# A fused conv and MLP layer on one core: T2 is put onto R21 by an adding transfer in the first two turns

## The reference, cut to what matters

```python
def short_conv_mixer(h, w_in, conv_w, w_out):
    b_gate, c_gate, v = jnp.split(h @ w_in, 3, axis=-1)
    u = c_gate * v
    y = lax.conv_general_dilated(u, conv_w[:, None, :], window_strides=(1,),
        padding=[(CONV_WIDTH - 1, 0)], dimension_numbers=('NWC', 'WIO', 'NWC'),
        feature_group_count=d)
    return (b_gate * y) @ w_out

def squared_relu_mlp(h, w1, w2):
    a = jax.nn.relu(h @ w1)
    return (a * a) @ w2

x = x + short_conv_mixer(rmsnorm(x, mix_norm), conv_w_in, conv_w, conv_w_out)
x = x + squared_relu_mlp(rmsnorm(x, mlp_norm), mlp_w1, mlp_w2)
```

## Time and profile before

| | us |
|---|---|
| median of 3 runs | 1921.16 |
| lowest, highest | 1919.78, 1921.49 |
| the profiled execution, its own time | 1920.67 |
| its span, first to last instruction | 1918.9 |
| PE busy | 1888.6 |
| DVE busy | 1713.0 |
| ACT busy | 1024.4 |
| POOL busy | 152.4 |

### The profile page before, as it was taken

One profiled execution on the slowest core, in us unless ns is written; L12 is line 12 of the kernel. 1 busy time (PEld: TensorE's weight loads), 2 busy tenths in 40 slices (PEclk: granted clock), 3 DMA queues, 4 the chain that ended last, 5 costly groups with the idle time before them and its releaser, 6 DMA issues.

```text
span 1918.9 us, 22282 instructions
## 1 busy us (share of the span) xinstructions
PE 1888.6 (98%) x8512; PEld 1562.5 (81%) x8512; DVE 1713.0 (89%) x1510; ACT 1024.4 (53%) x1102; POOL 152.4 (8%) x244
## 2 busy tenths in 40 slices
PE   6999999999999999999999999999999999999999
PEld 5778888888888888888888888888888888888887
DVE  7989899898999989989899898998998889888878
ACT  6753655536557486565665656655444333333332
POOL 1100001000011111111111111110000000000000
PEclk9999999999999999999999999999999999999999
DMA  9866659657776975967858678599988878877782
GB/s 361 307 208 171 224 173 376 214 158 263 243 198 245 376 221 182 335 243 238 318 185 331 247 235 322 183 397 400 362 311 348 351 284 310 349 317 277 296 329 116
DMA packets 120698, 527.90 MB, mean 275 GB/s; under 512 B 13072, under 2 KB 17168, under 8 KB 95504
## 3 DMA queue, kind: packets, MB, share of 16 engines
q1 hardware_dynamic: 86176, 401.64, 54.5%
q0 software_dynamic: 34272, 124.80, 21.4%
q10 hardware_dynamic: 144, 0.04, 0.0%
HBM read 433.10 MB, written 93.32 MB: 274 GB/s over the span
## 4 chain that ended last, share of the span: by engine, by line
PE 91%; DVE 4%; ACT 2%; issue 2%; DMA 1%; POOL 0%; ACTq 0%; DVEq 0%
PE pair L1014 89%; PE pair L1034 2%; DVE ring L787 1%; DVE raw L781 1%; DMA act_kept<-act 1%; ACT ring L545 1%; DVE act L744 1%; DVE sum_l_mix L818 0%; ACT quads L497 0%; DVE sum L816 0%; ACT act L530 0%; DVE sum_first_mix L827 0%; DMA quads<-in_xt 0%; ACT u_pad L608 0%; ACT sum L571 0%
## 5 line engine op out<-in xcount | busy, mean ns | idle before, releaser
L1014 PE MATMUL pair<-ring,act 128*128 128x512 f32 x8064 | 1851.8, 391 | 23.5 <-DVE ring L787 17.5
L1014 PEld LDWEIGHTS pair<-ring,act 128*128 128x128 f32 x8064 | 1512.5, 188 | 340.0 <-issue 21.6
L545 ACT ACTIVATE ring<-raw 128x1024 fp32r<-128x1024 f32 x672 | 710.8, 1060 | 833.0 <-PE pair L1014 563.1
L787 DVE TENSOR_TENSOR ring<-raw,ring 128x1024 fp32r<-128x1024 f32 x672 | 808.5, 1220 | 149.3 <-ACT ring L545 146.7
L781 DVE TENSOR_TENSOR raw<-raw 128x1024 f32<-128x1024 f32 x324 | 381.7, 1219 | 8.0
L432 POOL DMA_DIRECT2D spill<-stage x136 | 78.2, 609 | 474.9 <-ACT stage L649 371.6
L445 POOL DMA_DIRECT2D raw<-in_turns x60 | 53.5, 1045 | 780.5 <-DVE raw L781 780.5
L768 DVE TENSOR_TENSOR stage<-quads,stage 128x1024 fp32r<-128x1024 f32 x68 | 82.9, 1219 | 25.7 <-ACT stage L649 25.0
L818 DVE TENSOR_TENSOR sum<-pair,sum 128x1024 f32<-128x1024 f32 x64 | 77.9, 1217 | 0.0
L649 ACT ACTIVATE stage<-quads 128x1024 fp32r<-128x1024 f32 x68 | 71.4, 1051 | 11.8 <-DVE quads L716 10.1
L571 ACT ACTIVATE sum<-pair 128x1024 f32<-128x1024 f32 x64 | 64.7, 1011 | 0.0
(11 more groups left out here) (91 smaller groups left out, 438.3 us busy)
## 6 DMA issues: line engine op xcount, KB each, us to landing
raw<-in_turns SPq DMA_DIRECT2D x192, 1024.0 KB, 7.2
act<-spill SPq DMA_DIRECT2D x282, 512.0 KB, 6.7
spill<-stage POOLq DMA_DIRECT2D x136, 512.0 KB, 9.2
act<-act_kept SPq DMA_DIRECT2D x68, 512.0 KB, 7.1
raw<-in_turns POOLq DMA_DIRECT2D x60, 512.0 KB, 8.6
act_kept<-act POOLq DMA_DIRECT2D x26, 512.0 KB, 11.2
x_tok<-in_x SPq DMA_DIRECT2D x4, 1024.0 KB, 12.7
x<-mixed SPq DMA_DIRECT2D x8, 512.0 KB, 16.1
```

What stands on the lines that cost most here:

```text
L545: nc.scalar.activation(ring[g % RING][:, 0], raw[:, RAW_OF[j], 2 * (s % 2):2 * (s % 2) + 2, :], ACT.Copy).then_inc(hi_ready, 1)
L787: nc.vector.tensor_tensor(ring[g % RING][:, 1], raw[:, RAW_OF[s // 2], 2 * (s % 2):2 * (s % 2) + 2, :], ring[g % RING][:, 0].bitcast(F32), ...
L1014: mm = nc.tensor.matmul(bank, stationary, moving, start=(opens and k == 0 and n == 0), stop=(closes and k == NT - 1 and n == 2))
```

## The change

A fourth kind of transfer is added. In turns 0 and 1 (`t4_by_transfer`) POOL issues, behind the kept copies of the turn, two transfers of 512 KB that read T2 from R11 in `raw` and add it onto R21 in `raw`, so that both ends are on the chip. They wait for T2 and for lo of slot 7. Each half has a semaphore, `t4_in0` and `t4_in1`. DVE's two operations for T4 are left out in these turns. Hi of slots 12 and 13 waits for the half that it reads, and SP's load of the next turn's R11 waits for both halves. All other turns stay as they are, only the count of formed sums is adapted.

```diff
+def t4_by_transfer(v):
+
+    return v < 2
...
+        t4_in = [sem("t4_in0"), sem("t4_in1")]
...
-            before = sum(3 if t3_by_transfer(w) else 4 for w in range(v))
+            before = sum(4 - t3_by_transfer(w) - t4_by_transfer(w) for w in range(v))
...
                     if r == R11:
-                        sp.wait_ge(t_formed, formed(v, T4))
+                        if t4_by_transfer(v):
+                            for half in range(2):
+                                sp.wait_ge(t4_in[half], 16 * (v + 1))
+                        else:
+                            sp.wait_ge(t_formed, formed(v, T4))
                         load_raw(after, r)
...
+            def add_t4(v):
+
+                pool.wait_ge(t_formed, formed(v, T2))
+                pool.wait_ge(lo_ready, SLOTS * v + 8)
+                for half in range(2):
+                    k = slice(2 * half, 2 * half + 2)
+                    pool.dma_start(raw[:, R21, k], raw[:, R11, k], accum_op=ALU.add).then_inc(t4_in[half], 16)
...
                     keep_act(3, S2, S4, L22)
+                if t4_by_transfer(v):
+                    add_t4(v)
                 if v > 1:
                     put_spills(v)
...
+                elif j == L22 and t4_by_transfer(v):
+                    act.wait_ge(t4_in[s % 2], 16 * (v + 1))
                 elif j == S3 and t3_by_transfer(v):
...
-                    if s == 7:
+                    if s == 7 and not t4_by_transfer(v):
                         form_weights(v, T4)
```

## The result

The changed kernel took 1923.36 us (median of 20 runs, 1922.27 to 1926.28), the kernel before 1920.90 us in the same comparison (20 runs, 1919.48 to 1922.78). The ratio is 1.0013, 95% interval 1.0008 to 1.0019: 2.5 us slower, a difference that 20 runs show but that is under the 0.2% (3.8 us) named in the prediction. The profiled execution of the changed kernel took 1922.53 us, its span is 1920.8 us.

A forecast was written before the change was run, and what follows sets the result against it. PE, 98% busy, was taken as the bound, following DVE from turn 1 to the start of turn 2. Terms -1.8, +2.4 and +2.1 gave +2.7 us on 1920.67, so 1923.4, forecast as median 1923.9; range 1918.1 to 1929.2.

The forecast's parts named there:

- within 0.2%: Whole kernel: a time within 0.2% (3.8 us) of the kernel before, given a chance of 0.60.
- the three terms: Turns 0 to 2: -1.8 (kept copies), +2.4 (R12 behind tokens), +2.1 (R11 of turn 2), together +2.7 us.
- The second term: Turn 0 into turn 1: R12, behind 2 MB of tokens, lands at 65.7 and holds up T1; +2.4 us.
- the price of an addition: New transfers in turns 0 and 1: each adding transfer of 512 KB was taken to cost 2.9 us in the queue.
- The sign that would have refuted the prediction: PE's slot 4 of turn 2 starting before 119; it was forecast at 120.2, from 117.47.
- The step that the argument hung on: Turn 1 into 2: R11 of turn 2, issued at 96.4, lands at 101.2; DVE's list behind comes 2.7 us later.
- The first: Rival for turns 0 and 1: additions cost 1.25 us each like copies; -3.1 us, 1918.1 us; chance 0.08.
- The second: Rival for turns 0 and 1: SP waits for dearer additions; at 4.2 us each +7.9, 1929.1 us; chance 0.33.
- Its rate: Four additions ahead of the next R11: each 0.1 us more on an addition is 0.4 us on the kernel.
- The third: Rival in turn 2: PE's slot 4 may not be its only bound; sum near 0, 1921.2 us; chance 0.12.

The follow-up runs named there:

- e1: The changed kernel with T4 by transfer in turn 0 alone; 1922.67 us against 1921.49 for the kernel before, ratio 1.0005.
- e5: The changed kernel with four of turn 1's kept copies moved behind T3's transfers of turn 2; 1921.17 us against 1921.03 before, ratio 0.9999.
- e3: The changed kernel with turn 0's two token loads behind R21 instead of R11; 1923.85 us against 1921.49 before, ratio 1.0014.
- e4: The kernel before, with only SP's load of R11 of turn 2 held until lo of slot 12 of turn 1; 1923.26 us against 1921.49, ratio 1.0011.
- e10: The kernel before, with a semaphore for each operand's pair of kept copies of turn 0; 1919.52 us against 1921.00, ratio 0.9991.
- e8: The changed kernel with T4 by transfer in turn 1 alone and four kept copies moved to turn 2; 1919.98 us against 1921.03 before, ratio 0.9995.
- e9: The four new transfers copy T2 over R21 instead of adding it, leaving out the sum; 1919.27 us against 1921.03 for the kernel before, ratio 0.9988.
- e11: e8 plus a semaphore for each pair of kept copies of turn 0; 1918.96 us against 1921.00 for the kernel before, ratio 0.9990.

## Why the prediction was right, point by point

**The sum.** +2.7 us were forecast; the medians say +2.5, the profiled executions +1.9 (1922.53 to 1920.67). The median was forecast as 1923.9 and is 1923.4, inside the range and inside "within 0.2%". The path was as forecast, term by term, but that the number is so close is in part luck. Counted from lo of slot 4 of turn 0, the three terms were -1.68, +1.21 and +1.64 in the changed kernel's trace, for -1.8, +2.4 and +2.1. They give +1.17, and the other 0.56 us at slot 4 of turn 2 is the later start of slot 4 of turn 0 in this execution. The second term is not steady: in e1 and e5, whose turn 0 is the same, R12 landed 1.4 and 1.3 us later in the turn, and the term was +2.7 and +2.6.

**Turn 0.** The kept copies did speed up once SP held its loads back: the last landed at 48.1 (issued at 39.5, 8.6 us), 47.7 was forecast, 53.5 before. ACT's wait went from 3.37 to 1.66, and ended at 52.44, when `direct_s` was done (51.13 + 1.23 = 52.36; the row itself names only "issue"), as the prediction said. The additions landed at 50.6 and 53.05 (50.6 and 53.5), R12 at 65.3 (65.7), DVE stood 1.32 us for it, and T1 of turn 1 started at 65.28 (65.8; 65.19 before). PE's slot 12 was at 58.30, not 57.6; lo of slot 4 of turn 0 was already 0.56 later in this execution (31.76 to 31.20). e3 and e1 show both halves of the account: 1.2 us less without the tokens ahead of R12, and the gain gone with them.

**Turn 1.** The last kept copy, issued at 73.8, landed at 90.2 (90.5), the additions at 92.7 and 95.2 (93.4 and 96.3). The **cost that was mis-sized is the price of an addition**, 2.5 us and not 2.9: four of them make 1.6 us, but the first pair shows in T1 only in part. The 2.9 came from one pair of T3 in one execution; in e4 and e10, which leave that pair as it is in the kernel before, it was 2.5. R11 was issued at 95.25 and landed at 100.1 (96.4, 101.2), lo of slot 0 started at 101.25 (102.2), lo of slot 4 at 117.92 (118.9), PE's slot 4 at 119.20 (120.2). The sign that would have refuted the prediction, a start before 119, was close.

**The step that the argument hung on**, that the late load of R11 and not the waits on slots 12 and 13 sets the end of turn 1, is shown by e4: with the load alone 42.9 us, with the whole change 42.8, and the same 17.8 us from hi of slot 0 to lo of slot 4. That VectorE's saving is worth 1.3 us and no more if nothing is late is shown by e5, e8, e9 and e11: 41.2 became 39.9 each time.

**The rivals.** The first, additions as cheap as copies, was wrong about the additions; the sum given for it, -3.1 at the join, came near, as e9 showed by making them copies: 113.42 at slot 4 of turn 2, 2.8 us ahead of before; of this the median kept 1.8. The second, dearer additions, did not come: they were cheaper than in either row of T3, with SP's loads held back. Its rate, 0.4 us on the kernel for each 0.1 us, has only the two ends of e9 and the changed kernel behind it: 4.2 us (each against its own before) for 1.25 us less on each, so 0.34 for each 0.1. The third, a delay that doesn't reach the end, fell: ACT's wait before `sum_l_mix` stayed (0.63 for 0.67), and the 1.73 us at slot 4 of turn 2 became 1.86 at the end.

The Trainium skill's fit for a transfer ("DMA: Bandwidth & Descriptors", "Anatomy of one DMA — SWDGE (gpsimd) path"), with 1.2 us of data for 512 KB, holds for e9's copies (1.2 us apart) and not for the additions (2.5).

## What to carry to other kernels

Moving work from a full engine to a transfer also moves the release of the buffers it reads: ask who loads into them next, and add the whole way from the last landing through the next load to the first user. A transfer issued last in a shared queue lands when the queue is empty, so what is queued ahead of it counts like its own size: in turn 1 the pair landed 4.5 us earlier in its turn without the four copies (e5) and 3.2 earlier as plain copies (e9), and the stage was 39.9 both times. Moving a few copies that nobody needs yet behind it turned this change from a loss of 1.6 us in its turn into a gain of 1.3. And a wait on a count of all copies, where one pair would do, is worth a semaphore of its own before any work is moved: 1.5 us by the medians of e10, just at the edge of what its runs can tell from nothing.

## What the runs showed of the hardware that was not expected

An adding transfer with both ends on the chip costs the same in the queue as one whose source is in HBM, 2.5 us for 512 KB, twice a plain copy (1.2 us). A pair with hardly anything ahead of it landed after 6.0 and 8.0 us in e5, as T3's did before (6.4 and 8.7). The kernel before shows what such a transfer takes beyond that: its plain stores of 512 KB by POOL (`spill<-stage`) landed 2.9 us after issue at the soonest, its additions of T3 6.3 at the soonest. And moving 2 MB of token loads 7 us later, to a stretch that looked idle (e3), cost 1.1 us more in the stages of its trace than it gave, as it met the copies that followed.
